# A hybrid decoder layer with expert retrieval: seven input-projection columns behind the first expert scores, more free ring slots, output products in quarters, one norm moved

## What is computed

```python
h = x + concat[A, B, C, D](rmsnorm(x) @ W_in) @ W_out
y = h + PEER(rmsnorm(h))          # then a final rmsnorm

def peer_block(xb, eb, gb):       # 128 tokens, 8 heads x 16 experts each
    hsel = einsum('tsd,td->ts', u_tab[eb], xb)
    wgt = gb * gelu(hsel)
    return einsum('ts,tsd->td', wgt, v_tab[eb])
```

## Time and profile before

| | us |
|---|---|
| median of 3 runs | 1668.81 (1665.96 to 1669.25) |
| profiled execution, its own time | 1664.82 |
| its span in the profile | 1662.6 |
| TensorE busy | 1258.3 (76%) |
| VectorE busy | 1240.9 (75%) |
| ScalarE busy | 709.6 (43%) |
| GpSimd busy | 882.0 (53%) |

### The profile page before, as it was taken

One profiled execution on the slowest core, in us unless ns is written; L12 is line 12 of the kernel. 1 busy time (PEld: TensorE's weight loads), 2 busy tenths in 40 slices (PEclk: granted clock), 3 DMA queues, 4 the chain that ended last, 5 costly groups with the idle time before them and its releaser, 6 DMA issues.

```text
span 1662.6 us, 19427 instructions
## 1 busy us (share of the span) xinstructions
PE 1258.3 (76%) x5360; PEld 615.2 (37%) x5360; DVE 1240.9 (75%) x2947; ACT 709.6 (43%) x2021; POOL 882.0 (53%) x1135
## 2 busy tenths in 40 slices
PE   8998888776676888667977767777767776768665
PEld 6887755322233444333423323232223232323110
DVE  3878767788879888677788787767676776667776
ACT  3322224555454444344445644434344434434444
POOL 0364022767657666555567665555555554645552
PEclk9999999777887989788998777676877777877666
DMA  7321468999999999999999999999999999999996
GB/s 210 123 89 51 86 221 309 404 417 418 414 420 378 417 417 417 416 410 416 373 417 420 417 419 417 418 417 417 418 419 416 394 414 419 414 408 416 416 419 264
DMA packets 109307, 605.42 MB, mean 364 GB/s; under 512 B 22904, under 2 KB 25336, under 8 KB 42640
## 3 DMA queue, kind: packets, MB, share of 16 engines
q0 software_dynamic: 74880, 545.29, 80.0%
q1 hardware_dynamic: 34304, 58.89, 10.8%
q10 hardware_dynamic: 16, 0.02, 0.0%
HBM read 600.97 MB, written 3.19 MB: 363 GB/s over the span
## 4 chain that ended last, share of the span: by engine, by line
DMA 42%; PE 23%; DVE 16%; ACT 6%; POOL 6%; issue 4%; DVEq 3%; POOLq 0%
DMA arena<-in_uv,arena 42%; DVE arena L1982 8%; PE ps L1011 7%; PE ps L612 4%; DVE arena L1416 3%; DVEq L1413 3%; POOL arena L2236 3%; POOL arena L2235 2%; PE ps L962 2%; PE ps L684 2%; PE ps L981 2%; DVE arena L1422 1%; ACT arena L1343 1%; ACT arena L1339 1%; PE ps L663 1%
## 5 line engine op out<-in xcount | busy, mean ns | idle before, releaser
L1011 PE MATMUL ps<-arena 128*64 128x512 f32 x2048 | 677.6, 773 | 280.9 <-ACT arena L1343 279.4
L1982 DVE CUSTOM_DVE_ANT_0 arena<-arena 128x1024 f32<-128x1024 f32 x520 | 640.8, 1235 | 281.8 <-DMA arena<-in_uv,arena 260.0
L2236 POOL DMA_INDIRECT arena<-in_uv,arena x520 | 588.7, 1132 | 87.4 <-POOL arena L2235 16.3
L2235 POOL TENSOR_TENSOR arena<-arena 1x1 f32<-1x1 f32 x520 | 210.6, 405 | 526.3 <-PE ps L1011 445.4
L1337 ACT ACTIVATE arena<-arena 128x1 f32<-128x1 f32 x520 | 105.2, 202 | 702.7 <-DVE arena L1982 691.3
L1011 PEld LDWEIGHTS ps<-arena 128*64 128x64 f32 x2048 | 133.2, 161 | 692.2 <-ACT arena L1343 583.0
L1343 ACT ACTIVATE arena<-arena 128x64 f32<-128x64 f32 (+1 forms) x520 | 181.5, 349 | 16.9
L1339 ACT ACTIVATE arena<-arena 128x1 f32<-128x1 f32 x520 | 153.2, 295 | 16.9
L1416 DVE TENSOR_TENSOR arena<-arena 128x512 f32<-128x512 f32 (+9 forms) x312 | 134.7, 433 | 23.0 <-ACT arena L1095 8.8
L962 PEld LDWEIGHTS ps<-arena 128*128 128x128 f32 x1024 | 133.2, 214 | 39.1 <-issue 38.1
L612 PE MATMUL ps<-arena 128*128 128x264 f32 (+1 forms) x608 | 142.2, 389 | 0.3 <-DVE arena L1416 0.3
(11 more groups left out here) (177 smaller groups left out, 954.2 us busy)
## 6 DMA issues: line engine op xcount, KB each, us to landing
arena<-in_win SPq DMA_DIRECT2D x38, 512.0 KB, 3.3
arena<-in_wqk SPq DMA_DIRECT2D x60, 256.0 KB
arena<-in_wout SPq DMA_DIRECT2D x24, 512.0 KB, 5.4
arena<-in_uv,arena POOLq DMA_INDIRECT x520
arena<-in_xp SPq DMA_DIRECT2D x4, 512.0 KB, 6.2
out_yp<-arena SPq DMA_DIRECT2D x4, 512.0 KB
arena<-in_wqk SPq DMA_DIRECT2D x15, 128.0 KB
arena<-in_const SPq DMA_DIRECT2D x1, 864.0 KB, 7.1
```

The source lines that it names most:

```text
L1011: last = mm(ps[64 * c:64 * c + 64, b + s % 2, :], diag[:, s % 8, :], ring[:, SLOT_OF[k], D + 512 * c:D + 512 * c + 512], start=(s < 2 and ...
L1982: v.tensor_tensor_reduce(out=here, in0=here, in1=row, scale=1.0, scalar=0.0, op0=MUL, op1=ADD, accum_out=hsel[:, u % 2, s:s + 1]).then_inc ...
L2235: pool.tensor_tensor(carrier[:, 1:2], carrier[:, 0:1], carrier[:, 0:1], ALU.add).then_inc(S["carried"], 1)
L2236: pool.indirect_dma_start(out=ring[:, SLOT_OF[k], :], out_offset=None, in_=a["uv"][:, :], in_offset=bass.IndirectOffsetOnAxis(ap=idx[:, t, ...
```

## The change

Of the seven late z columns none stands any more among the output blocks of tile 0: `BLOCKS` ends with the output blocks. The seven have five buffers (`zlate` two, and the three `ASIDE` places after their use) and semaphores of their own. Output blocks 6 and 7 of tile 0 have two more buffers, loaded earlier. Slots 0 to 6 are free at the first gather instead of five; slot 7 becomes free when all z columns are copied. The second half of the short convolution moves from GpSimd to VectorE, behind tile 0's transposes. Nine taps leave the end of the front, three come in behind the square and six among the first dots. The conf layernorm of group 1 moves behind the first dots on VectorE, TensorE and ScalarE. The output product of tiles 2, 3 and the samples goes in four pieces per tile instead of two. In the last unit tile 3's final norm stands after the eighth dot.

```diff
-SLOT_OF = [0, 1, 2, 3, 4, 0, 1, 2, 3] + [(5, 6, 7, 4, 0, 1, 2, 3)[k % 8] for k in range(8 * 65)]
-FREE = (0, 1, 2, 3, 4, 9, 10, 11)
-FRESH = 9
+SLOT_OF = 2 * list(range(7)) + [0, 1] + [(7, 2, 3, 4, 5, 6, 0, 1)[k % 8] for k in range(8 * 65)]
+FREE = (0, 1, 2, 3, 4, 5, 6, 16)
+FRESH = 16
-Z_HIGH = 35
+Z_HIGH = 33
+EARLY = 6
-BLOCKS = z_blocks(0, ZFRONT) + out_blocks(0, 0, 2) + z_blocks(ZFRONT, ZFRONT + 1) + out_blocks(0, 2, 6) + z_blocks(ZFRONT + 1, ZFRONT + 2) \
-    + out_blocks(0, 6, 8) + out_blocks(1, 0, 5) + z_blocks(ZFRONT + 2, len(ZORDER))
+BLOCKS = z_blocks(0, ZFRONT) + out_blocks(0, 0, EARLY) + out_blocks(1, 0, 5)
...
# SyncE
-                if n == n_out - 2:
+                if n == n_out - 6:
+                    sp_.dma_start(w_early[0], a["wout"][:, OUT_ORDER[EARLY], :]).then_inc(d_early[0], 16)
+                elif n == n_out + 2:
+                    sp_.wait_ge(d_swkv, 16)
+                    sp_.dma_start(w_early[1], a["wout"][:, OUT_ORDER[EARLY + 1], :]).then_inc(d_early[1], 16)
...
-                k = n - n_out - 8
+                k = n - n_out - 5
...
-                elif k == 5:
-                    sp_.wait_ge(S["short_done"], 2)
-                    for i, j in enumerate(ASIDE):
-                        sp_.dma_start(w_aside[i], a["wout"][:, OUT_ORDER[j], :]).then_inc(d_aside, 16)
+            sp_.wait_ge(S["short_done"], 2)
+            for i, j in enumerate(ASIDE):
+                sp_.dma_start(w_aside[i], a["wout"][:, OUT_ORDER[j], :]).then_inc(d_aside, 16)
...
             sp_.wait_ge(S["tails_done"], 3)
+            for i in range(2):
+                late_weights(i)
...
+            sp_.wait_ge(S["out_mm"], 2)
+            for i in range(2, 5):
+                late_weights(i)
+            for i in range(5, len(ZORDER) - ZFRONT):
+                sp_.wait_ge(S["z_done"], ZFRONT + i - 4)
+                late_weights(i)
# TensorE
                 for k in range(3):
-                    yield C_OUT + 7 * k
-                    project(k, 0)
-                    yield C_OUT + 7 * k + 4
-                    project(k, 1)
+                    for piece in range(4):
+                        yield C_OUT + 7 * k + (0, 2, 4, 5)[piece]
+                        project(k, piece // 2, piece % 2)
...
             first_out(0, 0, 2)
-            zcol()
             first.finish()
...
             first_out(0, 2, 6)
-            zcol()
             pe.wait_ge(S["rwkv_out"], 1)
             first_out(0, 6, 8)
             first_out(1, 0, 1)
-            conf_mean(1)
...
             query(0)
-            conf_variance(1)
             score(0)
             first_out(1, 1, 8)
-            zcol(3)
+            zcol()
             turned(1, 0)
             turned(1, 1)
+            zcol()
             query(1)
             score(1)
             pe.wait_ge(S["z_copied"], Z_HIGH)
             sums(0, 0)
             sums(0, 1)
-            zcol()
+            zcol(2)
+            conf_mean(1)
             sums(0, 2)
             sums(0, 3)
+            zcol(2)
+            sums(0, 4)
+            sums(0, 5)
+            conf_variance(1)
             zcol()
# ScalarE, first unit
-                    if k == 5:
+                    if k in (4, 5, 7):
+                        zc()
+                    if k == 7:
+                        conf_root(1)
+                    if k == 9:
                         conf_sigmoid(1)
# VectorE
-                taps(3)
+                taps(3 if c < GC - 1 else 0)
             first.until(C_LN + 2)
-            taps(64)
+            taps(3)
...
             second_features(0, 1)
-            conf_center(1)
+            short_second()
...
                     if k == 4:
-                        for step in range(STEPS - 1):
+                        for step in range(6, STEPS - 1):
                             choose(1, step)
+                    elif k == 5:
+                        conf_center(1)
                     elif k == 7:
                         choose(1, STEPS - 1)
                     elif k == 8:
+                        conf_scale(1)
+                    elif k == 11:
                         conf_swish(1)
...
-                    if ended and s == (15 if u < NU else 3):
+                    if ended and s == (15 if u < NU else SLOTS_S - 1):
                         final_norm(ended[0])
...
-            conf_scale(1)
             residual(1)
...
             dot(0, 1)
+            taps(3)
             dot(0, 2)
+            taps(64)
             dot(0, 3)
+            for step in range(6):
+                choose(1, step)
# GpSimd
-            short(1)
+            pool.wait_ge(S["short_done"], 2)
...
+                    elif k == 5:
+                        pool.wait_ge(S["block_used"], KT - 1 + 5)
```

More of the change, by code:

```diff
@@ L845, in mixer, with project @@
                 tiles = (2, 3, TILES)
-                def project(k, nh):
+                def project(k, nh, part):
                     t = tiles[k]
-                    if not nh:
+                    if not nh and not part:
                         pe.wait_ge(S["rwkv_out"], 2)
@@ L1052, in unit @@
                     return
-                for s in range(4 if u == 0 else 0, TOPK):
+                for s in range(6 if u == 0 else 0, TOPK):
                     sums(u, s)
@@ L1326, in _ @@
             queries(0)
-            conf_root(1)
             act.wait_ge(d_const, 16)
```

78 lines of the change are left out of this document (52 added, 26 removed).

## The result

The changed kernel took 1673.24 us (median of 6 runs), the kernel before beside it 1666.74 us (6 runs): a ratio of 1.0037 with a 95% interval of 1.0024 to 1.0050, 6.2 us **slower**. The prediction was 4 us faster, and 1673.24 lies above its range. One run of the six took 2114.8 us; the ratio leaves it out. The profiled execution took 1673.62 us, its span is 1671.8 us (before 1664.82 and 1662.6).

What follows compares the result with a forecast made beforehand. The prediction took the DMA's gathers of expert rows, 1304 of 1662.6 us, as the bound. Front 2.1, quarters 1.0 and norm 0.8 made 3.9, say 4.0 us off 1668.81: 1664.8, range 1657.5 to 1672.

Steps and rivals of the forecast that it cites:

- The front up to the gated output: Group 0's last norm to its gated output: fewer slow taps bring the output to 221.7, 7.5 us earlier.
- Part 1: The way to the first gather: it goes out at 250.2 instead of 258.16, 8.0 us earlier.
- From there to the score copy all steps stay: Tile 0 after output blocks 6 and 7: step times unchanged, less some 0.4 us; score copy at 238.0.
- Part 2, tile 1: Tile 1's output blocks, norm, query and score: first sums at 270.8 against 277.62, 6.8 us earlier.
- the columns run at half clock: Rival: five z columns and a query at 1.2 GHz cost 8 us more; 0.03, within the slower case.
- The start slips: Rival: late short convolution or block loads put the first gather at 253; 2 us slower than forecast, 1666.5; chance 0.13.
- Part 3, the ring: Gathers up to the twentieth: z column pairs delay free slots, gaps 9.3 us, leaving 2.1 of 8.0 us gained.
- VectorE waits for that until about 299.9 just as before: VectorE's wait for unit 1's softmax on ScalarE: ends about 299.9, as before at 299.97.
- Slower, VectorE and ScalarE behind: Rival: dots fall behind and the DMA runs dry again up to gather 40; some 7.5 us over forecast, 1672.3; chance 0.20.
- The bytes of the late columns: Late z column weights still loading once gathers run: three more columns of bytes than before, 3.8 us of DMA.
- Quarters and norm: Output products of tiles 2 and 3 in quarters gain 1 us; tile 3's norm behind the last dot gains 0.8.
- The base: Time the gain was taken off: the shown median 1668.81, less 4.0 us, gives 1664.8.

Runs made afterwards that it cites:

- filled_tile0: Changed kernel plus eight spare products of unread values on TensorE, only around tile 0's transposes; 1669.39 us, ratio 1.0016 to the kernel before.
- no_late_loads: Changed kernel with z columns 33 to 37 reusing the weights of columns 31 and 32, five late loads left out; 1673.46 us, ratio 1.0041 to the kernel before.
- warm_blocks: Changed kernel with output block 1 of tile 1 moved in front of tile 0's transposes; 1670.01 us, ratio 1.0030 to the kernel before.
- q_alone: Kernel before with only the output products in quarters; 1664.55 us, ratio 0.9994 to the kernel before.
- norm_alone: Kernel before with only tile 3's final norm moved behind the last unit's eighth dot; 1663.64 us, ratio 0.9987 to the kernel before.

## Why the prediction was wrong

The sum was: start 8.0 us earlier, of which 2.1 are left after gaps of 9.3 us; quarters 1.0; norm 0.8. Point by point:

- **The front up to the gated output was right.** VectorE's first reciprocal starts at 215.37 (forecast 215.65), the gated output ends at 221.45 (221.7), the six taps behind the square take 2.79 us (2.8). The Trainium skill (SBUF — State Buffer, "SBUF: two separate sides") has a VectorE instruction with two SBUF inputs wait for the shared ports only against a GpSimd instruction that reads SBUF; the trace agrees: 2.79 us with GpSimd idle, 6.93 us beside its convolution. The short convolution on VectorE ends at 238.3, well before the score copy, at no cost.
- **Part 1 failed at "From there to the score copy all steps stay".** Blocks 6 and 7 came near their time (forecast 226.5, the residual behind them at 227.76), but query 0 took 6.39 us instead of 3.81. I took the duration of a matmul group from the trace of before without asking what had kept TensorE busy in front of it: the mean product of group 1 directly ahead of the transposes, which the change moves, and further ahead the z columns, whose removal I booked as a gain. Which of the two matters was not run. With 1.2 us of lateness of the blocks ahead of it (waits of 0.81 and 1.46 us for their weights, and the residual on their heels), the score copy came at 242.12 instead of 238.0, and the first gather at 254.5 instead of 250.2. Mending the clock there (`filled_tile0`, where column 32 gained 1.5 us too) is worth 3.5 us by the ratios, with about 3 us of noise.
- **Part 2, tile 1, failed by the same step and by it again.** First sums at 278.63 instead of 270.8. Of these 7.8 us 4.3 come from tile 0 and 2.5 from column 32 (6.13 instead of 3.63); the rest is small. The output blocks' wait was forecast at 3.6 us and was 2.2 (0.33 and 1.84).
- **The rival "the columns run at half clock" looked in the wrong place.** It counted 8 us for five columns and a query from 264 to 302 and got 0.03. In that stretch the five columns ran at 3.6 us each, as forecast. Its price was also too low: 1.4 us for a column or a query, where query 0 lost 2.6 and column 32 2.5. I cited the Trainium skill (TensorE: Matmul & The Clock Gate, "What's actually happening") for the clock staying up there. The same section says that the low level is the resting state and that activity lifts it; applied to the sparse stretch before 234 it would have been a warning. The trace agrees with it there: busy 4.74 of 8 us, then a granted clock of 0.50; and filled, 7.77 of 8 us and 1.00.
- **"The start slips"** (0.13) had a first gather at 253 or later, and it came at 254.5. But its cause, a late convolution or late blocks, makes up only 1.2 of the 4.3 us, and its price of 2 us was too small, since it left the ring as forecast.
- **Part 3, the ring, was right in its mechanism and wrong in its size.** I foresaw pairs of columns in front of the sums and slots coming free in twos; the distance was 10.0 us from one release to the next (281.03 to 291.06), against 9.0 forecast. What failed is "VectorE waits for that until about 299.9 just as before": it waited until 308.97. I had put the seventh sum at 297 and it came at 304.95, 8 us late, which is the lateness of the first sums handed on by a TensorE that has no idle time to absorb it. In the DMA rate the gaps from 285 to 330 are 50 us at 292 GB/s from 280 on, 6.3 MB or 15 us instead of 9.3. The start came 4.3 us later than forecast and the gaps were 5.7 us longer: 10 of the 10.6 to 11.5 us between the 2.1 us gained that I forecast for the front and the 8.5 to 9.4 us lost.
- **"Slower, VectorE and ScalarE behind" had the right sign, and its point of decision was passed** (gaps past 16.5 us would be slower by over 0.2%, it said; with the first gather 4.3 us later than forecast the 15 us measured are beyond it). Its mechanism was not what happened: VectorE was not behind by its own work but idle, 11.96 us, and from 350 to 400 the DMA moved 418 GB/s. It had 0.20.
- **The bytes of the late columns**, 3.8 us of DMA in my sum, cost nothing that could be measured: `no_late_loads` is at 1.0041. They fell into gaps that were there anyway. My sum added DMA work and DMA idle time as if neither could hide the other.
- **Quarters and norm had the right sign**: 1.0 us forecast for the quarters and 1.0 measured, with the rate at 805 rising to 419 GB/s; since the interval reaches from 2.8 us faster to 0.8 slower, that the numbers meet is luck. 0.8 was forecast for the norm and 2.2 measured; the interval, 0.7 to 3.8, holds both the forecast and the bound of 1.2 that I had set, and the last dots show 1.2.
- **The base.** I took 4.0 us off 1668.81, the median of three runs; over six runs it is 1666.74. The 8.4 us between 1664.8 and 1673.24 therefore make the miss look 2 us smaller than it is: 4.0 us gained were forecast and 6.2 lost.

Sum by measured parts: quarters -1.0, norm -2.2 (or -2.3 for both with the early softmax), so +8.5 to +9.4 for the front against -2.1 forecast. The spare products take 4.3 of it away, the spread columns with the early softmax 6.8, both together 10.3. Each of these ratios has an interval of about 2 us to either side, so that whether they overlap by 1 us isn't known.

Open: what exactly brings the clock down. In the kernel before, idle times of 1.04 us before and behind the transposes leave query 0 at full speed; in `warm_blocks` 1.10 and 1.04 us at the same places leave it at 5.44 us. The busy share ahead of the query does not tell them apart: 5.27 of 8 us before, 5.86 in `warm_blocks`. The spare products show that filling the idle times brings the clock back (7.60 of 8 us busy and 1.00), not how little would do. Whether a spread order without spare products can hold the clock was not tried either.

## What to carry to other kernels

When a change takes filler work off an engine with a gated clock, price the work that follows at both clock levels: list the idle times that the removed or moved work leaves ahead of it, and do not trust the busy share to decide between the levels, since here it did not. When a ring feeds a DMA-bound stretch, follow the release times of its slots before you credit an earlier start: an earlier first transfer moved nothing in the old ring, and what counted in the new one was how much of an in-order engine's work stood in front of the releases. Work that is due later belongs there one piece at a time, as far back as its deadline allows. And compare the bytes moved up to a common point beyond the disturbed stretch: among the changed kernel and those made from it with every load kept, the spans fall as the rate to 350 rises, from 1671.8 us at 185 GB/s over 1669.1 and 1669.7 at 187, 1667.8 at 189, 1665.2 to 1667.7 at 191, 1664.1 at 193 and 1663.3 at 195 to 1658.1 at 200.

## What the runs showed of the hardware that had not been expected

- Work added for nothing but its activity made the kernel faster: 16 products of 0.46 us, and 4.3 us less by the ratios, with about 3 us of noise.
- Query 0's 32 matmuls took 3.81 us at 2.4 GHz and 5.21 to 6.67 us where the clock fell to 1.2 GHz before or early in them; z column 32 took 3.63 and up to 6.13 us. Idle times of 0.9 to 2.8 us around short transposes preceded them; 1.10 and 1.04 us went with the lower clock in one kernel (5.44 us), 1.04 and 1.04 us did not in another, though it had been busy for less of the 8 us before.
- With a 0.5 MB store issued shortly before the last dots the last two lie 3.7 and 3.6 us apart (kernel before, `q_alone`), with the store behind them 2.5 us (`norm_alone`, changed kernel), and the end came no later for it.
